# The order of outputs, transposes and copies in the second mixer of a two-block transformer kernel

## The chip, the cores and the metric

The kernel runs on one core of a Trainium2 chip. The metric is device time in microseconds of one execution. Before the change the median of three runs is 2345.12 us (2344.96 to 2345.4).

## The reference

Two transformer stacks run one after the other on one stream of 512 tokens of 1024 features. The first stack has two layers and also carries 256 context tokens, which are dropped after the last layer. Each of its layers has three attention mixers side by side, A, B and C, then a gate and an output product. Mixer B, the one that matters here, has 8 heads of 64 features. Each latent query sees a neighbourhood of 8 rows by 16 columns of latent keys with a learned bias, and all 256 context keys, in one softmax:

```
s_nb  = q . k_gathered + bias
s_ctx = q . k_context
p = softmax_f32(concat([s_nb, s_ctx]))
y = p[:neighbours] @ v_gathered + p[neighbours:] @ v_context
```

Context queries see only the context keys, and only in layer 0. The second stack (another attention, retention, convolution, pooling, and a feed-forward part) is not touched by the change.

## The kernel before, in words

Everything is written out by hand: each engine has its own loop over the same plan, and semaphores tie the queues together. A queue works strictly in its own order, so that order is the subject here.

Per layer, `project` makes the tiles of a mixer, then the mixer's attention runs over units. A unit is 128 queries of two heads. In mixer B a band unit has 512 keys a head (256 of context and a band of 256 latent ones), a context unit 256. `band_units` gives four band units for each of four pairs of heads, `context_units` two context units more in layer 0. That is 24 units in layer 0 and 16 in layer 1. A group is the units of one pair of heads: six and four.

`make_plan` turns the units into steps. The step of unit i names three of them: `unit` is i, `prev` is i-1, `old` is i-2. It also names up to one transpose of values for the coming pair of heads, which is done beside the transposes of `prev` (four, four and two tiles of 128 in three of the steps of a group; none in the last group). For `prev` the two halves of the partitions are transposed by pairs of 64-row matmuls: eight pairs for a band unit (16 matmuls), four for a context unit, and as many more as there are value tiles.

TensorE (`attention_pe`, L745) does in a step: `scores_pe` (matmuls at L621) of unit i; the transposes of unit i-1 (`turn_halves_pe`, L645, matmuls at L671), which first wait for both of its exponentials; and `outputs_pe` (L718) of unit i-2, which spreads the row weights (L715), then waits for the copy of the transposes and multiplies with the values (L730).

VectorE (`attention_dve`, L890): row minima with the bias added (L837, for context units L832), the copy of transposed probabilities (no unit of mixer B has any for VectorE), the reciprocal of the row sums (L855), the values copy (L888), then the product of outputs and weights (`outputs_dve`, L857: L862, L873).

ScalarE (`attention_act`, L940): in mixer B the two exponentials of unit i (`exponentials_act`, L928, activation at L937) come first and the copy of the transposes of unit i-1 (`turned_act`, L909, L926) last; `copies_last` is true where a unit has a set of two banks, which is mixer B alone. In mixers A and C the copy comes first. The exponentials write a buffer that the transposes of the unit before read, so they wait for them (L933 to L935). GpSimd only starts the loads of the bias behind the row minima (L958, L961).

Scores sit in three sets of two banks of PSUM in turn, transposes go into the banks of their own unit's scores, outputs have bank 1 and value transposes bank 0. The first two steps of a mixer run inside the last projection, and behind the last two there is one chunk of the next mixer's projection each (`latents_ahead`, L781, L790).

Of the kernel before, what the change touches and what calls it, by code (L numbers as in the profile page):

```python
# [226 lines left out]
def two_dit_blocks(nc, dram, kept, out):  # L227
    with ExitStack() as ctx:
# [478 lines left out]
        def spread_weights_pe(pe, u, o):  # L707

            if u["i"] >= 1:

                pe.wait_ge(y_done, u["u"] + o.u)
            pe.wait_ge(weight_ready, u["u"] + 1 + o.u)
            s, b = 2 * u["i"] % 4, u["out_bank"]
            for e in range(2):
                nc.tensor.matmul(bank(b, P, 2 * P)[rows_of(e)], weight[:, s + e:s + e + 1].to_broadcast([P, HD]), ident,  # L715
                                 start=True, stop=True, skip_group_check=True)

        def outputs_pe(pe, u, o):  # L718

            b = u["out_bank"]  # L720
            pe.wait_ge(values_taken, u["values_seen"] + o.w)
            spread_weights_pe(pe, u, o)
            for ev in u["events"]:
                if ev["by"] == "act":
                    pe.wait_ge(pt_by_act, ev["c"] + 1 + o.act)
                else:
                    pe.wait_ge(pt_by_dve, ev["c"] + 1)
                tiles = places(ev)
                for j, (at0, _, e, v) in enumerate(tiles):
                    ins = nc.tensor.matmul(bank(b, 0, P)[rows_of(e)], v, turned_slot(ev, at0 + P)[:, at0:at0 + P],  # L730
                                           start=ev["first"] and j < 2, stop=ev["last"] and j >= len(tiles) - 2,
                                           skip_group_check=True)
                ins.then_inc(pv_steps, 1)
# [11 lines left out]
        def attention_pe(pe, l, m, o, early):  # L745

            last = PHASES[m][1] - 1
            steps = plans[l, m][0]
            n_early = 2 if m == "B" else 1
            for step in steps[:n_early] if early else steps[n_early:]:  # L750
                u, prev, old = step["unit"], step["prev"], step["old"]
                i = u["i"] if u else None
                if i == 1 and m != "C":

                    pe.wait_ge(mod_taken, panels_through(l, m))
                if m == "B" and i == 2:

                    pe.wait_ge(proj_taken, NSEQ[l, last] + 1)
                if m == "A" and i == 1:

                    pe.wait_ge(proj_taken, NSEQ[l, last])
                if m == "B" and i == 2:

                    pe.wait_ge(values_taken, steps[0]["values"][1]["w"] + 1)
                if u and m in "AC" and u["p"] > 0:

                    pe.wait_ge(rope_done, rope_no(l, m, 1 + u["p"]) + 1)
                if u and not (m == "C" and i == 1):
                    scores_pe(pe, u, o)
                if u is None and old:  # L770
                    latents_ahead(pe, l, NEXT[m], 0 if prev else 1)
                if prev:
                    turn_halves_pe(pe, prev, [ev for ev in step["values"] if ev["halves"]])
                if m != "B" and i == 1:

                    pe.wait_ge(proj_taken, NSEQ[l, last] + 1)
                turn_values_pe(pe, step, o)
                if old:
                    outputs_pe(pe, old, o)

        def latents_ahead(pe, l, m, c):  # L781


            b = PHASES[m][0]
            k, n = NSEQ[l, b], main_no[IN1, l, b]
            if c == 0:
                pe.wait_ge(rest1_done, n + 1)
                pe.wait_ge(proj_taken, k - 1)
            for i, (w, h) in enumerate(((0, 0), (0, 1), (1, 0))):
                nc.tensor.matmul(bank(k % 2), split1[:, n % SPLIT1, w, c, :], hs1[:, h, c, 0:SEQ], start=c == 0 and i == 0, stop=False)  # L790
# [60 lines left out]
        def weights_dve(dve, u, o):  # L851

            s = 2 * u["i"] % 4
            dve.wait_ge(exp_done, 2 * u["u"] + 2 + o.u * 2)
            nc.vector.reciprocal(weight[:, s:s + 2], row_sum[:, s:s + 2]).then_inc(weight_ready, 1)  # L855

        def outputs_dve(dve, u, o):  # L857

            V = nc.vector
            dve.wait_ge(pv_steps, u["events"][-1]["k"] + 1 + o.k)  # L860
            a, f, d = bank(u["out_bank"], 0, P), y_weights[:, :], u["dst"]
            V.tensor_copy(f, bank(u["out_bank"], P, 2 * P))  # L862
            dve.drain()
            if len(d.shape) == 3:
                a, f = (x.rearrange("p (c r) -> p c r", r=ROWS) for x in (a, f))
            if "rest" in u:
                V.tensor_tensor(f, a, f, ALU.mult)
                dve.drain()
                V.tensor_copy(d, f)
                dve.drain()  # L870
                V.tensor_tensor(u["rest"], f, d.bitcast(F32), ALU.subtract).then_inc(y_done, 1)
            else:
                V.tensor_tensor(d, a, f, ALU.mult).then_inc(y_done, 1)  # L873

        def values_dve(dve, step, o, halves=False):

            for ev in step["values"]:
                if ev["halves"] != halves:
                    continue
                dve.wait_ge(turned, ev["t"] + 1 + o.t)  # L880
                if ev["after"]:

                    dve.wait_ge(pv_steps, ev["after"]["events"][-1]["k"] + 1 + o.k)
                to, of = ev["dst"], bank(ev["bank"], 0, P * len(ev["src"])).rearrange("p (t c) -> p t c", c=P)
                if ev["halves"]:
                    to = to.rearrange("p t (h q) -> p h t q", h=2)
                    of = bank(ev["bank"]).rearrange("p (h t q) -> p h t q", h=2, q=HD)[:, :, 0:len(ev["src"]), :]
                nc.vector.tensor_copy(to, of).then_inc(values_taken, 1)  # L888

        def attention_dve(dve, plan, o, behind_first=None):  # L890

            for step in plan:
                u, prev, old = step["unit"], step["prev"], step["old"]
                if u:
                    maxima_dve(dve, u, o)
                    if behind_first and u["i"] == 0:
                        behind_first()
                if prev:
                    turned_dve(dve, prev, o)
                    weights_dve(dve, prev, o)  # L900
                values_dve(dve, step, o, halves=True)
                if u and step["values_first"]:
                    values_dve(dve, step, o)
                if old:
                    outputs_dve(dve, old, o)
                if u is None or not step["values_first"]:
                    values_dve(dve, step, o)

        def turned_act(act, u, o):  # L909

            for ev in u["events"]:
                if ev["by"] == "act":
                    n = P * 2 * len(ev["tiles"])
                    if u["parts"]:
                        act.wait_ge(first_turned, u["x_no"] + 1)
                    else:
                        act.wait_ge(turned, ev["t"] + 1 + o.t)
                    if "slot_before" in ev:

                        act.wait_ge(pv_steps, ev["slot_before"]["k"] + 1 + o.k)  # L920
                    to, both = copy_of_turned(ev, n)
                    if u["parts"]:
                        nc.scalar.copy(to[:, 0], both[:, 0])
                        act.wait_ge(turned, ev["t"] + 1 + o.t)
                        to, both = to[:, 1], both[:, 1]
                    nc.scalar.copy(to, both).then_inc(pt_by_act, 1)  # L926
# [13 lines left out]
        def attention_act(act, plan, o, early=False):  # L940


            for step in plan:
                u, prev = step["unit"], step["prev"]
                copies_last = u and len(u["set"]) == 2
                if prev and not copies_last:
                    turned_act(act, prev, o)
                if u and not (early and u["i"] == 0):
                    exponentials_act(act, u, o)
                if prev and copies_last:  # L950
                    turned_act(act, prev, o)

        def attention_pool(pool, plan):

# [1588 lines left out]
        def _(pe):  # L2543
# [352 lines left out]
            for l in range(DEPTH):  # L2896
                for m in "ABC":
                    project(l, m)
                    attention_pe(pe, l, m, zero, False)
# [457 lines left out]
```

## Time and profile before

| what | us |
|---|---|
| median of three runs | 2345.12 |
| the profiled execution's own time | 2343.62 |
| its span, first to last instruction | 2341.8 |
| mixer B, layer 0, first transposes to last | 286.04 to 347.00 |
| mixer B, layer 1, second unit's transposes to last | 894.39 to 935.50 |

The profile is of one execution. PE is TensorE's matmuls and PEld its weight loads, which run ahead of them; DVE is VectorE, ACT ScalarE, POOL GpSimd. L and a number is a line of the kernel. Where TensorE has waited, its first matmul starts with its weight load; where it has not, the matmul follows the load by some 0.2 us.

### The profile page before, as it was taken

What the parts mean: (1) busy time and instruction counts of PE and PEld (TensorE: products, weight loads), DVE (VectorE), ACT (ScalarE), POOL (GpSimd) and SP (SyncE); (2) the same over time, 40 slices, a digit from 0 to 9 for tenths busy, and PEclk for the clock granted to TensorE, in tenths of its full rate; (3) what the DMA queues carried; (4) which work ended last, traced back from release to release, by engine and by line L of the source; (5) the groups of instructions that cost most, each with busy time, mean ns of one, the idle gap of its engine ahead of it and who ended that gap; (6) DMA issues with size and microseconds to landing.
All of it is one profiled execution on the core that took longest, in us unless ns stands there. A gap on an engine that the chain in (4) does not pass through costs nothing.

```text
span 2341.8 us, 39975 instructions
## 1 busy us (share of the span) xinstructions
PE 2300.3 (98%) x15942; PEld 1902.9 (81%) x15942; DVE 1401.3 (60%) x2818; ACT 1011.9 (43%) x1750; POOL 464.9 (20%) x291
## 2 busy tenths in 40 slices
PE   8999999999999999999999999999999999999998
PEld 7878878788888888888887688888888768888887
DVE  5878776787136766453388558847857755333333
ACT  5773375723247527653455442222235535221221
POOL 2102212022441131214752420000014232000001
PEclk9999999999999999999999999999999999999999
DMA  7303413042222151112241125445442112323222
GB/s 308 143 2 145 171 47 127 2 189 98 67 92 78 59 198 57 55 64 90 86 157 62 56 91 198 167 148 185 170 142 82 55 54 90 100 78 112 99 83 70
DMA packets 64201, 250.51 MB, mean 107 GB/s; under 512 B 7408, under 2 KB 9968, under 8 KB 54544
## 3 DMA queue, kind: packets, MB, share of 16 engines
q1 hardware_dynamic: 61216, 236.10, 29.0%
q0 software_dynamic: 2592, 11.54, 1.5%
q8 instruction: 126, 2.06, 0.4%
q14 instruction: 59, 0.48, 0.1%
q10 hardware_dynamic: 208, 0.33, 0.0%
HBM read 243.67 MB, written 4.19 MB: 106 GB/s over the span
## 4 chain that ended last, share of the span: by engine, by line
PE 89%; ACT 4%; DVE 3%; issue 2%; DVEq 1%; DMA 1%; POOL 1%; ACTq 0%; SPq 0%
PE ps L2948 41%; PE ps L2744 13%; PE ps L2729 8%; PE ps L2925 6%; PE ps L621 4%; PE ps L730 4%; ACT probs L937 3%; PE ps L671 3%; PE ps L715 1%; PE ps L2758 1%; PE ps L2965 1%; PE ps L2615 1%; DMA stage_low<-in_ada 1%; DVEq L820 1%; PE ps L2781 1%
## 5 line engine op out<-in xcount | busy, mean ns | idle before, releaser
L2948 PE MATMUL ps<-h_split,split_panels 128*128 128x512 f32 x2088 | 500.0, 394 | 1.2 <-ACT projected L1788 0.8
L2948 PEld LDWEIGHTS ps<-h_split,split_panels 128*128 128x128 f32 x2088 | 387.9, 188 | 92.8 <-issue 14.7
L1251 POOL TENSOR_TENSOR split_panels_first<-panels_first,split_panels_first 128x1024 fp32r<-128x1024 f32 (+2 forms) x100 | 220.8, 2208 | 728.9 <-ACT split_panels_first L1468 728.9
L2744 PE MATMUL ps<-h_split_first,split_panels_first 128*128 128x256 f32 (+1 forms) x1680 | 294.4, 337 | 0.0
L2744 PEld LDWEIGHTS ps<-h_split_first,split_panels_first 128*128 128x128 f32 x1680 | 258.3, 190 | 34.3 <-issue 1.0
L1269 POOL TENSOR_TENSOR probs_turned<-probs_turned,probs 128x512 f32<-128x512 f32 x30 | 40.0, 1332 | 764.3 <-ACT probs L1731 761.7
L2729 PE MATMUL ps<-h_split_first,split_panels_first 128*128 128x512 f32 (+1 forms) x900 | 190.5, 370 | 0.9 <-POOL h_split_first L1290 0.9
L2729 PEld LDWEIGHTS ps<-h_split_first,split_panels_first 128*128 128x128 f32 x900 | 156.3, 189 | 32.4 <-issue 3.0
L2243 DVE TENSOR_TENSOR split_panels<-panels,split_panels 128x1024 fp32r<-128x1024 f32 (+2 forms) x110 | 127.7, 1164 | 89.0 <-ACT split_panels L1493 88.9
L1920 ACT ACTIVATE probs<-ps 128x512 f32<-128x512 f32 x44 | 26.3, 599 | 349.8 <-PE ps L2948 349.7
L1493 ACT ACTIVATE split_panels<-panels 128x1024 fp32r<-128x1024 f32 (+2 forms) x149 | 144.7, 979 | 67.0 <-PE ps L2948 63.0
L2051 DVE SCALAR_TENSOR_TENSOR ps<-modulation_panels,silu_c,ps 128x256 f32<-128x256 f32 x312 | 145.5, 487 | 19.0 <-issue 1.3
L2948 PE MATMUL ps<-ffn_hidden_split,split_panels 128*128 128x512 f32 x624 | 145.7, 389 | 0.0
L621 PE MATMUL ps<-qkv 64*128 64x256 f32 (+1 forms) x1232 | 144.6, 360 | 0.3
L1468 ACT ACTIVATE split_panels_first<-panels_first 128x1024 fp32r<-128x1024 f32 (+2 forms) x104 | 102.5, 986 | 97.9 <-PE ps L2925 96.0
L937 ACT ACTIVATE probs<-ps,row_min 128x512 f32<-128x512 f32 (+6 forms) x192 | 122.2, 644 | 38.7 <-DVE row_min L837 29.0
L2948 PEld LDWEIGHTS ps<-ffn_hidden_split,split_panels 128*128 128x128 f32 x624 | 117.1, 188 | 24.3
L2925 PE MATMUL ps<-gated_rounded,split_panels_first 128*128 128x512 f32 x504 | 132.9, 356 | 0.0
L1281 POOL TENSOR_TENSOR split_panels<-panels,split_panels 128x1024 fp32r<-128x1024 f32 x39 | 94.5, 2423 | 169.3 <-ACT split_panels L1493 167.8
L621 PEld LDWEIGHTS ps<-qkv 64*128 64x128 f32 x1232 | 98.9, 186 | 25.9 <-issue 18.1
L671 PEld LDWEIGHTS ps<-matrices,probs 64*128 64x128 f32 x2048 | 80.6, 138 | 43.1 <-ACT probs L937 37.5
L1553 ACT ACTIVATE qkv<-ps 128x512 f32<-128x512 f32 x38 | 37.1, 975 | 167.2 <-PE ps L2744 118.0
(341 smaller groups left out, 3964.7 us busy)
## 6 DMA issues: line engine op xcount, KB each, us to landing
panels<-in_w SPq DMA_DIRECT2D x88, 512.0 KB, 3.7
modulation_panels<-in_ada SPq DMA_DIRECT2D x40, 1024.0 KB, 4.9
panels_first<-in_in SPq DMA_DIRECT2D x72, 512.0 KB, 4.8
late_modulation_panel<-in_ada SPq DMA_DIRECT2D x24, 1024.0 KB, 4.8
panels<-in_in SPq DMA_DIRECT2D x42, 512.0 KB, 3.7
panels_first<-in_out SPq DMA_DIRECT2D x32, 384.0 KB, 3.1
panels<-in_w SPq DMA_DIRECT2D x32, 384.0 KB, 3.5
panels<-in_w SPq DMA_DIRECT2D x32, 320.0 KB, 2.9
```

The lines of the kernel that those rows point to most:

```text
L621: last[e] = nc.tensor.matmul(scores_at(u, e, u["w"][e])[:, col:col + z - a], u["q"][e], u["k"][e][:, a:z], start=True, stop=True, skip_gro ...
L671: ins = [nc.tensor.transpose(to, src, ident[rows_of(half), HD * half:HD * half + HD]) for half, (to, src) in enumerate(two)]
L937: nc.scalar.activation(probs[:, u["probs_at"], e, 0:w], scores_at(u, e, w), ACT.Exp, bias=row_min[:, s:s + 1], scale=scale, accum_out=row_ ...
L1251: nc.gpsimd.tensor_tensor(flat1(n, 1)[:, s], raw1[:, n % RAW1, s], flat1(n, 0)[:, s].bitcast(F32), ALU.subtract).then_inc(rest1_done, 1)
L1468: A_(flat1(n, 0)[:, s], raw1[:, n % RAW1, s], ACT.Copy).then_inc(rounded1, 1)
L1493: A_(flat(n, l, 0), raw[:, n % RAW, 0:panel_size(n)], ACT.Copy).then_inc(rounded, 1)
L2051: ins = V.scalar_tensor_tensor(out=adding if c < KC - 1 else made[:, PAN * i:PAN * i + PAN], in0=w[:, c, :], scalar=v, in1=adding, op0=ALU ...
L2243: V.tensor_tensor(flat(n, l, 1), raw[:, n % RAW, 0:panel_size(n)], flat(n, l, 0).bitcast(F32), ALU.subtract).then_inc(rest_done, 1)
L2729: ins = mm(at0, split1[:, s, w, c, :], hs1[:, h, c, lo:e], start=c == 0 and i == 0, stop=c == KC - 1 and i == 2)
L2744: ins = mm(to, split1[:, s, w, c, :], hs1[:, h, c, lo:lo + n], start=c == 0 and i == 0, stop=c == KC - 1 and i == 2)
L2925: ins = mm(bank(OUT_BANKS[j][o % 2], 0, e), split1[:, n % SPLIT1, w, c, :], u[:, uc, lo:lo + e], start=uc == 0 and i == 0, stop=uc == MIXC ...
L2948: ins = mm(out, panel_of(n, l)[:, a, c - base, :], moving(b, c), start=first and i == 0 and j == 0, stop=last and i == len(chunks) - 1 and ...
```

## The change

In mixer B's steps three queues get another order. On TensorE the outputs of `old` come between the scores and the transposes. On VectorE the product of the outputs comes ahead of the values copy. On ScalarE the copy of the transposes comes ahead of the exponentials, as in the other mixers.

```diff
@@ attention_pe
                 if u is None and old:
                     latents_ahead(pe, l, NEXT[m], 0 if prev else 1)
+                if old and m == "B":
+                    outputs_pe(pe, old, o)
                 if prev:
                     turn_halves_pe(pe, prev, [ev for ev in step["values"] if ev["halves"]])
...
                 turn_values_pe(pe, step, o)
-                if old:
+                if old and m != "B":
                     outputs_pe(pe, old, o)
@@ attention_dve
                     weights_dve(dve, prev, o)
+                outputs_first = old and old["in_sets"] and len(old["set"]) == 2
+                if outputs_first:
+                    outputs_dve(dve, old, o)
                 values_dve(dve, step, o, halves=True)
...
-                if old:
+                if old and not outputs_first:
                     outputs_dve(dve, old, o)
@@ attention_act
-                copies_last = u and len(u["set"]) == 2
-                if prev and not copies_last:
+                if prev:
                     turned_act(act, prev, o)
                 if u and not (early and u["i"] == 0):
                     exponentials_act(act, u, o)
-                if prev and copies_last:
-                    turned_act(act, prev, o)
```

## Rows read from the trace of the kernel before

**Rows 1.** The page: busy us, share of the span, instructions of each engine.

```profile
PE 2300.3 (98%) x15942; PEld 1902.9 (81%) x15942; DVE 1401.3 (60%) x2818; ACT 1011.9 (43%) x1750; POOL 464.9 (20%) x291
```

**Rows 2.** By stretch: length, busy PE, PEld, DVE, ACT, POOL, granted clock, DMA.

```profile
396.00:480.00 84.00, 79.24 (x1136) 65.41 (x1137) 59.97 (x222) 55.48 (x124) 2.88 (x2) 1.00 0.05 17
284.00:346.00 62.00, 60.43 (x928) 49.37 (x926) 44.89 (x150) 48.34 (x116) 5.93 (x11) 1.00 0.18 52
886.00:935.00 49.00, 48.29 (x738) 41.45 (x735) 36.40 (x117) 36.88 (x79) 4.88 (x9) 1.00 0.20 59
```

**Rows 3.** Waits of PEld, mixer B in layer 0, then 1: total, times, longest.

```profile
PEld ps L671 <- ACT probs L937: 5.0, 11, 1.1
...
PEld ps L671 <- ACT probs L937: 1.5, 2, 1.1
```

**Rows 4.** Timeline, mixer B: group starts, and one step: start, us, engine, instruction.

```profile
300.73 0.73 PEld L621 LDWEIGHTS ps<-qkv 64*128 64x128 f32 x8 [0.17 <-issue]
...
316.77 0.73 PEld L621 LDWEIGHTS ps<-qkv 64*128 64x128 f32 x8 [0.17 <-issue]
...
338.47 0.73 PEld L621 LDWEIGHTS ps<-qkv 64*128 64x128 f32 x8 [0.17 <-issue]
...
340.02 0.20 PEld L715 LDWEIGHTS ps<-matrices,row_weight 128*64 128x64 f32 x4
...
341.15 0.68 ACT L937 ACTIVATE probs<-ps,row_min 128x512 f32<-128x512 f32 x1
341.26 0.30 PEld L621 LDWEIGHTS ps<-qkv 64*128 64x128 f32 x4 [0.17 <-issue]
```

**Rows 5.** Timeline, mixer B, the first two transposes, with values beside them.

```profile
286.04 0.14 PEld L671 LDWEIGHTS ps<-matrices,probs 64*128 64x128 f32 x1
...
288.81 0.13 PEld L671 LDWEIGHTS ps<-matrices,probs 64*128 64x128 f32 x1 [1.11 <-ACT probs L937]
...
289.73 0.20 PEld L715 LDWEIGHTS ps<-matrices,row_weight 128*64 128x64 f32 x4
...
289.93 0.69 ACT L937 ACTIVATE probs<-ps,row_min 128x512 f32<-128x512 f32 x1 [0.26 <-PE ps L671]
```

**Rows 6.** Timeline, mixer C in layer 0, where the copy stands ahead of the exponentials.

```profile
408.94 0.83 PE L671 MATMUL ps<-matrices,probs 64*128 64x64 f32 x20 [0.48 <-ACT probs L937]
...
409.84 1.01 ACT L926 COPY probs_turned<-ps 128x1024 f32<-128x1024 f32 x1 [0.95 <-PE ps L671]
...
410.75 0.70 ACT L937 ACTIVATE probs<-ps,row_min 128x513 f32<-128x513 f32 x1
...
411.43 0.69 ACT L937 ACTIVATE probs<-ps,row_min 128x513 f32<-128x513 f32 x1
...
412.26 0.71 PE L671 MATMUL ps<-matrices,probs 64*128 64x64 f32 x16
...
413.04 1.01 ACT L926 COPY probs<-ps 128x1024 f32<-128x1024 f32 x1 [0.83 <-PE ps L671]
```

**Rows 7.** Timeline, mixer B: context units and end in layer 0; layer 1.

```profile
345.13 0.47 ACT L937 ACTIVATE probs<-ps,row_min 128x256 f32<-128x256 f32 x1 [0.40 <-DVE row_min L832]
...
345.60 0.46 ACT L937 ACTIVATE probs<-ps,row_min 128x256 f32<-128x256 f32 x1
...
347.00 0.46 PE L671 MATMUL ps<-matrices,probs 64*128 64x64 f32 x8
...
347.39 0.20 PEld L715 LDWEIGHTS ps<-matrices,row_weight 128*64 128x64 f32 x4
...
347.53 0.59 ACT L926 COPY probs<-ps 128x512 f32<-128x512 f32 x1 [0.90 <-PE ps L671]
...
348.20 0.53 PEld L790 LDWEIGHTS ps<-h_split_first,split_panels_first 128*128 128x128 f32 x3 [0.17 <-issue]
...
894.39 0.27 PE L671 MATMUL ps<-matrices,probs 64*128 64x64 f32 x1 [0.71 <-ACT probs L937]
...
935.50 0.71 PE L671 MATMUL ps<-matrices,probs 64*128 64x64 f32 x16
```

## The prediction

> **What bounds the kernel now.** I read the busy shares first, then the busy time by stretch, then the waits inside the second mixer, then its timeline. TensorE is busy for 98% of the span [rows 1], and in the second mixer's two stretches for 60.43 of 62.00 us and 48.29 of 49.00 us, all at a granted clock of 1.00; ScalarE has 48.34 of 62 us of work there, so it is no bound by its sum [rows 2]. The only wait of TensorE that another engine causes in the mixer is that of the transposes for the exponentials: 5.0 us in 11 waits in the first layer, 1.5 us in 2 in the second [rows 3]. So before the change the stage is a chain of TensorE work with 6.5 us of holes, and 6.5 us is the most that filling these holes can bring. Any TensorE time that the change adds or removes here moves the end one for one, since what follows is TensorE-bound too.
>
> Names: S(i), T(i), O(i) are the scores, transposes and outputs of unit i on TensorE, E(i) its exponentials and C(i) the copies of its transposes on ScalarE. There are 24 units in layer 0 (four pairs of heads, each four band units of 512 keys and two context units of 256) and 16 in layer 1 (band units only), so 40 steps in all. The step of unit i has S(i), T(i-1), O(i-2) on TensorE and E(i), C(i-1) on ScalarE; after it, S(i), O(i-2), T(i-1) and C(i-1), E(i).
>
> **The change part by part.** It removes and adds no instruction; 40 steps are reordered on three queues, and no DMA is moved (POOL's band loads still follow the row minima).
>
> *TensorE's own price.* A band step without values beside it costs 341.26 - 338.47 = 2.79 us: S and T 1.55 us (338.47 to 340.02), spread weights and outputs 1.24 us (340.02 to 341.26) [rows 4]. The order of the three does not change that sum. T with twelve pairs (eight of probabilities, four of values) issues in 0.92 us [rows 5]; T with eight pairs by subtraction from S at about 0.76 in about 0.8, and tightly packed when it was waited for, about 0.64 (an estimate: 0.92 x 8/12).
>
> *ScalarE's order.* This is the part that decides. E(i) writes the same probs buffer that T(i-1) reads, and L933 to L935 already make E(i) wait for T(i-1); that wait is visible, ScalarE restarts 1.12 us after the first transpose (288.81 to 289.93) [rows 5]. Today C(i-1) comes behind E(i), off that path: the loop is T(i-1), E(i), T(i), 1.12 + 0.68 + 0.83 = 2.6 us, shorter than or equal to TensorE's own 2.8 to 3.2. With C(i-1) ahead of E(i) the loop is T(i-1), C(i-1), E(i), T(i), strictly serial. The third mixer already runs in this order, so its rows price each link [rows 6]: T with ten pairs to the copy 0.90 (408.94 to 409.84), with eight pairs 0.78 (412.26 to 413.04); copy of 1024 to the first exponential 0.91; first to second exponential of 513 columns 0.68; second exponential to the next transposes 0.83. Their sum there, 0.90 + 0.91 + 0.68 + 0.83 = 3.32, is exactly the distance of its two T (408.94 to 412.26). For context units the copy of 512 lasts 0.59 against 1.01 and the exponential of 256 0.47 against 0.69 [rows 6, 7]; I take copy to exponential 0.48, exponential to exponential 0.46, second exponential to transposes 0.61, and T with four pairs to the copy 0.53 (347.00 to 347.53) [rows 7].
>
> The loop from T(i-1) to T(i), for each unit i of a group in layer 0:
> - b0 after a context unit: 0.53 + 0.48 + 0.68 + 0.83 = 2.52
> - b1 and b2, T with twelve pairs (1.12 less the rounding): 1.11 + 0.91 + 0.68 + 0.83 = 3.53 each
> - b3, T with ten pairs: 0.90 + 2.42 = 3.32
> - c0: 0.78 + 0.91 + 0.46 + 0.61 = 2.76. Here another wait ends last: O(b3) now stands ahead of T(c0), and needs C(b3), which is done at 0.78 + 1.01 and about 0.07 for the signal; the outputs issue in 1.24 - 0.16 = 1.08, so T(c0) starts at 2.94
> - c1: 0.53 + 0.48 + 0.46 + 0.61 = 2.08
>
> A group of six: 17.92 us. Before it took 316.77 - 300.73 = 16.04 us [rows 4]. TensorE between two T has T, S, O: 0.64 + 0.76 + 1.24 = 2.64 (0.92 in place of 0.64: 2.92), below 3.20 and 3.53, so the loop rules and TensorE idles 0.5 to 0.6 us a band step. Does the wait of O(i-1) for C(i-1) add? It can start at 1.11 + 1.01 + 0.07 = 2.19 and issues to 3.27, still under 3.53; with eight pairs 1.86 + 1.08 = 2.94 under 3.20: no.
>
> Layer 0, from the first T: b1 to c1 of the first group 15.40; two whole groups 35.84; the last group has no values beside it, 2.52 + 3 x 3.20 + 2.94 + 2.08 = 17.14 (3.20 = 0.78 + 2.42). Sum 68.38. Before: 347.00 - 286.04 = 60.96 [rows 5, 7]. Cost +7.42.
>
> Layer 1: first group 3.53 + 3.53 + 3.32 = 10.38; two groups 3.20 + 10.38 = 13.58 each, 27.16; last group 4 x 3.20 = 12.80. Sum 50.34. Before: 2.77 for the first loop (286.04 to 288.81, the same instructions in layer 0) and 935.50 - 894.39 = 41.11 [rows 5, 7], 43.88. Cost +6.46.
>
> *TensorE's order* gives something back once per layer: O of the last unit but one no longer stands behind the last T. Layer 0: 348.20 - 347.39 = 0.81 [rows 7]. Layer 1: 1.24, less a new wait of the last outputs for the last copy, 0.78 + 1.01 + 0.07 against 0.64 + 0.9 of T and latents, 0.32: 0.92.
>
> *VectorE's order* is taken at nothing. O(i-2) is finished before T(i-1), so its product goes ahead of the values copy, which waits for T. The cover: S(i) starts 0.64 us after T(i-2), and both minima have served E(i) by 341.15 - 338.47 = 2.68 us after S began [rows 4]; E(i) now cannot begin before 3.20 + 0.78 + 0.91 = 4.9 after T(i-2), 4.25 after S(i). So up to 2.2 us of delay on VectorE is hidden. If that cover were gone, each late microsecond would add in its step. Bounds: 0 to +0.3 a group for the values copy of 0.69 us, which now stands last before the next minima, so 0 to +2 in all.
>
> Sum: 7.42 + 6.46 - 0.81 - 0.92 = +12.15 us on the profiled execution of 2343.62 us (span 2341.8 and 1.8 outside it). The median of the three timed runs is 1.5 us higher, 2345.12, so 2357.2 us.
>
> Bounds of the unknowns. The links come from another mixer with the same instructions; each is read to 0.05 us, and 38 loops with a common error of 0.1 make 3.8 us either way. The signal from copy to outputs (0.07) and the short-unit links are estimates worth 1 us. Low end 12 - 5.5, high end 12 + 6.
>
> A rule of the Trainium skill, beside this: "ScalarE: Activation LUTs", section "Rules for kernel authors", budgets about 0.3 us per activation and 0.83 ns an element, by which the copy of 1024 would take 1.15 us where the trace has 1.01 and lets the next instruction start after 0.91. By the page every loop would be some 0.24 us longer and the change would cost about 21 us; the measured row decides.
>
> **The rivals.**
> 1. *Faster: the holes are filled.* O(i-2) between S(i) and T(i-1) gives the exponentials 1.24 us more, and no wait seen is longer than 1.1 us. If the copies did not lengthen the way to E(i), all 6.5 us [rows 3] and both tails (0.81 + 1.24) would go: -8.6, 2336.5 us. For it: the waits are real and TensorE is the bound. Against: ScalarE's copy takes 0.91 of the 1.24, and it must wait for T(i-1), which itself has moved 1.24 later; the third mixer, in this order, waits at 408.94 and still takes 3.32 a step [rows 6]. It decides if the loop is under 2.8.
> 2. *No change.* Loop and TensorE's own time balance: that needs a loop of 2.9 us, 0.3 to 0.6 less than the third mixer shows. 2344 to 2346 us.
> 3. *Slower by more.* Copies and exponentials after each other cost more than in the third mixer, or the minima come late as well (the +2 above): a loop 0.24 longer, 38 x 0.24 = +9, 2366 us.
> 4. *TensorE's clock falls.* TensorE would idle about a sixth of the stage in holes of some 0.5 us. In the third mixer it is busy 79.24 of 84.00 us with its own such holes and the granted clock is 1.00 [rows 2]. If it fell to 1.2 GHz, TensorE's 2.8 us a step would be some 5.6, 40 x 2.3 = +92 over the stage, 2440 us. The Trainium skill, "TensorE: Matmul & The Clock Gate", section "A second HAM failure mode: psum-queue depth-cycling", tells of a kernel whose short idles between groups of matmuls made the clock swing; the trace, with such idles at full clock, speaks against it here.
>
> **How the numbers follow.** Forecast (slower by 7 to 18 us) 0.86; rival 1 0.05; rival 2 0.03; rival 3 0.05; rival 4 0.01. A measurement of this kernel tells about 0.2%, 4.7 us, from no change. Slower by over 0.2%: 0.92; within 0.2%: 0.03; faster by over 0.2%: 0.05. The range is the forecast's own with a little more at the low end, 2350.5 to 2363 us.
>
> **What would show it.** In the changed kernel's second mixer: the wait of transposes for exponentials grows from 6.5 us to some 20 (0.5 us a band step, 36 or so waits); ScalarE's idle before the copies is on TensorE's transposes and no longer on the minima; the copy starts 0.8 to 1.1 us after each T, and the distance of two T is 3.2 to 3.5 us; a group of six takes 17.9 us against 16.04. Mixers one and three, with the same queues as before, keep their lengths. I am wrong if a group takes under 16.0 us (then the copy was not on the loop), or if the waits of TensorE are on minima or on the copies (then the bound is another than I say).

## The result and the profile after

| | us |
|---|---|
| before, median of 5 runs | 2345.12 (2343.48 to 2345.47) |
| changed, median of 5 runs | 2355.29 (2355.08 to 2355.7) |
| ratio, 95% interval | 1.0046 (1.0035 to 1.0056) |
| span of the profiled execution | 2341.8 before, 2353.3 changed |

The change makes the kernel slower by 10.2 us; 12.1 were forecast. One execution of the kernel before, among those beside E5 to E8 below, took 4180.94 us at a granted clock of 0.82 and is left out of the ratios.

The page of the changed kernel shows next to nothing: TensorE is busy for the same 98% and its weight loads for the same 81%. The busy time of the matmuls even rose by 4.5 us with no matmul added; their ends are modelled, so the gaps below are read from the weight loads (PEld).

```profile
PE 2304.8 (98%) x15942; PEld 1898.4 (81%) x15942; DVE 1404.5 (60%) x2818; ACT 1011.5 (43%) x1750; POOL 465.0 (20%) x291
```

By stretch (length, then busy PE, PEld, DVE, ACT, POOL, granted clock, DMA), the second mixer of layers 0 and 1 in the changed kernel, against [rows 2]: TensorE idles 6.1 of 66 us and 3.1 of 47 us, where it was 1.6 of 62 and 0.7 of 49, at an unchanged clock.

```profile
284.00:350.00 66.00, 59.92 (x901) 44.41 (x902) 46.57 (x149) 47.26 (x111) 5.92 (x11) 1.00 0.16 46
893.00:940.00 47.00, 43.92 (x652) 34.55 (x652) 33.38 (x102) 31.96 (x67) 4.88 (x9) 1.00 0.19 58
```

The waits of layer 0's mixer in the changed kernel (who <- whom and line: total, times, longest), against [rows 3]: the transposes wait 23 times in place of 11, none longer than 0.5 us, and ScalarE's idle time is now that of its copies for the transposes, 24 times for 24 units. Before the change 10.2 us of ScalarE's idle time there were waits for minima; in layer 0 of the changed kernel there is none.

```profile
ACT probs_turned L931 <- PE ps L671: 10.0, 12, 1.1
ACT probs L931 <- PE ps L671: 9.9, 12, 1.1
...
PEld ps L671 <- ACT probs L942: 8.7, 23, 0.5
...
PEld ps L715 <- issue: 6.6, 19, 0.4
...
PEld ps L730 <- ACT probs_turned L931: 2.1, 4, 0.5
PEld ps L730 <- ACT probs L931: 2.1, 4, 0.5
```

The same wait in layer 1:

```profile
PEld ps L671 <- ACT probs L942: 7.4, 15, 0.5
```

Both layers together: 16.1 us in 38 waits, where the prediction had some 20 in about 36. The outputs (L730) wait for copies as well, 4.2 us in 8 waits in layer 0. The prediction called waits on the copies a sign that the bound is another; four of them are the wait into c0 that it had priced, and behind the other four the transposes still wait 0.50 us for the exponentials, so these do not end last.

The loop itself stands in the timeline (start, us, engine, instruction, idle time before it in brackets). This is one band step without values in the changed kernel, against [rows 4, 6]:

```profile
344.56 0.58 PEld L671 LDWEIGHTS ps<-matrices,probs 64*128 64x128 f32 x16 [0.50 <-ACT probs L942]
...
345.35 1.01 ACT L931 COPY probs_turned<-ps 128x1024 f32<-128x1024 f32 x1 [0.84 <-PE ps L671]
...
346.26 0.69 ACT L942 ACTIVATE probs<-ps,row_min 128x512 f32<-128x512 f32 x1
346.41 0.85 PEld L730 LDWEIGHTS ps<-probs_turned,mixed_first 128*64 128x64 f32 x16 [0.52 <-ACT probs_turned L931]
...
346.93 0.69 ACT L942 ACTIVATE probs<-ps,row_min 128x512 f32<-128x512 f32 x1
...
347.76 0.58 PEld L671 LDWEIGHTS ps<-matrices,probs 64*128 64x128 f32 x16 [0.50 <-ACT probs L942]
```

From transposes to copy 0.79, copy to first exponential 0.91, to the second 0.67, to the next transposes 0.83: 3.20 us. No minima stand in it, and no other wait of ScalarE.

Measured from one unit's transposes to the next (differences of such starts), with T, C, E, O, S as in the prediction:

| loop into unit | before | forecast | changed |
|---|---|---|---|
| b0 after a context unit | 2.75 | 2.52 | 2.52 |
| b1 of the first group, T with values | 2.77 | 3.53 | 3.63 |
| b1 of the next groups, T with values | 2.72 | 3.53 | 3.47 |
| b2, T with values | 2.94 | 3.53 | 3.47 |
| b3, T with fewer values | 2.74 | 3.32 | 3.32 |
| c0 | 2.25 | 2.94 | 2.87 |
| c1 | 2.64 | 2.08 | 2.12 |
| group of six | 16.04 | 17.92 | 17.77 |
| band units of the last group, no values | 2.34 to 2.94 | 3.20 | 3.19 or 3.20 |

First transposes to last, and last transposes to the next projection:

| | before | changed | difference | forecast |
|---|---|---|---|---|
| layer 0, T to T | 60.96 | 68.03 | +7.07 | +7.42 |
| layer 0, end | 2.90 | 2.09 | -0.81 | -0.81 |
| layer 1, T to T | 43.89 | 50.14 | +6.25 | +6.46 |
| layer 1, end | 4.11 | 2.87 | -1.24 | -0.92 |
| sum | | | +11.27 | +12.15 |

The difference of the two spans is 11.5 us. Outside the mixer the two profiled executions differ by -1.3 us in the first 35 us and +1.3 us at the seam of the layers, places that no edit touches. Mixers one and three keep their lengths.

### The profile page after: what moved, and what is told of

It reads as the page before. It is cut to its first block, busy times and chain, and to the rows that moved or that the text cites. A ratio compares the mean times of both kernels' runs of the same rounds, so it can differ in the third digit from the quotient of the medians.

```text
span 2353.3 us, 39975 instructions
## 1 busy us (share of the span) xinstructions
PE 2304.8 (98%) x15942; PEld 1898.4 (81%) x15942; DVE 1404.5 (60%) x2818; ACT 1011.5 (43%) x1750; POOL 465.0 (20%) x291
## 4 chain that ended last, share of the span: by engine, by line
PE 86%; ACT 6%; issue 3%; DVE 2%; DVEq 1%; DMA 1%; POOL 1%; ACTq 0%; SPq 0%
PE ps L2950 41%; PE ps L2746 12%; PE ps L2731 8%; PE ps L2927 6%; ACT probs L942 4%; PE ps L671 3%; PE ps L621 3%; PE ps L730 3%; PE ps L2967 2%; PE ps L2760 1%; PE ps L2617 1%; PE ps L715 1%; DMA stage_low<-in_ada 1%; DVEq L822 1%; PE ps L2783 1%
## 5 line engine op out<-in xcount | busy, mean ns | idle before, releaser
L671 PE MATMUL ps<-matrices,probs 64*128 64x64 f32 x2048 | 93.2, 228 | 20.9 <-ACT probs L942 19.0
```

What stands on the lines that cost most here:

```text
L671: ins = [nc.tensor.transpose(to, src, ident[rows_of(half), HD * half:HD * half + HD]) for half, (to, src) in enumerate(two)]
```

## Experiments

Each is told with its edit; times are medians beside runs of the kernel before on the same chip, and ratios have their 95% interval.

**E1, ScalarE's order alone.** On the kernel before:

```diff
-                copies_last = u and len(u["set"]) == 2
-                if prev and not copies_last:
+                if prev:
                     turned_act(act, prev, o)
                 if u and not (early and u["i"] == 0):
                     exponentials_act(act, u, o)
-                if prev and copies_last:
-                    turned_act(act, prev, o)
```

> The kernel before with ScalarE's order alone changed (mixer B's copy of transposes ahead of the next exponentials); TensorE and VectorE as before. Theory (serial loop transposes, copy, exponentials, transposes): the loop is there with TensorE's old order too. Layer 0 from first to last transposes about 67.6 us against 60.96 before, layer 1 about 50.1 against 43.9, and no gain at the ends since the last outputs stay behind the last transposes: 2345.1 + 6.7 + 6.3 = 2358 us, 2 to 3 us slower than the whole change. Rival (the cost is TensorE's new order, outputs waiting for copies ahead of the transposes): 2345 us, no change.

Measured 2359.65 against 2345.25 us, ratio 1.0068 (1.0054 to 1.0081). Between first and last transposes 69.61 and 50.19 us, ends 2.90 and 4.10 as before. The band loops are those of the whole change, 3.47, 3.48, 3.32, 3.20 in the same places. Waits of layer 0:

```profile
PEld ps L671 <- ACT probs L937: 15.7, 19, 2.0
ACT probs L926 <- PE ps L671: 11.6, 12, 1.1
ACT probs_turned L926 <- PE ps L671: 9.6, 12, 1.1
```

The rival is out: TensorE's new order is not needed for the loss. The 69.61 against the 67.6 expected lies in the short units: into b0 the loop is 2.75 and into c1 2.39, where I had carried over 2.52 and 2.08. There TensorE's own work, with outputs still behind transposes, is the longer of the two (the kernel before has 2.75 and 2.64). So TensorE's and VectorE's parts of the change, taken together, give some 4 us back (2359.65 to 2355.29).

**E2, VectorE's order alone.** The middle part of the diff, on the kernel before.

> The kernel before with VectorE's order alone changed (product of the outputs ahead of the values copy). Theory: covered; the values copy ends 0.5 us later and the next minima up to 0.2 us later, inside the slack of the transposes in steps of 2.9 to 3.2 us: 2345 us, 0 to +1. Rival (VectorE's order carries part of the cost): +2 or more.

Measured 2349.92 against 2345.25 us, ratio 1.0024 (1.0014 to 1.0034): slower by 4.7 us. The rival was right and I was not. T to T grows by 2.46 us (63.42) in layer 0 and by 2.87 (46.76) in layer 1, all of it behind transposes that have values beside them. In a whole group of layer 0 the loop into b1 goes from 2.72 to 3.21 and into b2 from 2.94 to 3.69, and the one into b3 falls from 2.75 to 2.47. The step into b2 in its timeline:

```profile
304.39 0.73 PEld L621 LDWEIGHTS ps<-qkv 64*128 64x128 f32 x8 [0.17 <-issue]
...
304.51 0.29 DVE L862 COPY weights_of_y<-ps 128x128 f32<-128x128 f32 x1 [0.60 <-PE ps L730]
...
305.08 0.68 DVE L888 COPY mixed_first<-ps 128x512 f32<-128x512 f32 x1
...
305.88 0.13 PEld L671 LDWEIGHTS ps<-matrices,probs 64*128 64x128 f32 x1 [0.76 <-ACT probs L940]
```

The name in the bracket is misleading: the exponentials had ended at 305.14 (304.46 and 0.68), the transposes start only 0.12 us after the values copy of the step before (305.08 and 0.68). All value transposes share one bank of PSUM, and `turn_halves_pe` waits for it ahead of all its pairs. The copy is late because the product of the outputs now stands ahead of it, and starts only at 304.51, when TensorE has done the outputs, which in this run still stand behind the transposes. In the whole change the outputs stand ahead of the transposes, the product is done in time, and the values copy starts 1.06 us after its transposes (288.33 to 289.39), 2.4 us before the next ones (291.80):

```profile
289.39 0.69 DVE L890 COPY mixed_first<-ps 128x512 f32<-128x512 f32 x1 [0.25 <-PE ps L671]
```

No loop there is longer than ScalarE's links explain. The whole change without VectorE's part was not run. I had looked for the delayed minima and not for the bank.

**E3, TensorE's and VectorE's order without ScalarE's.** The changed kernel with the old `attention_act`.

> The changed kernel with ScalarE's order put back (exponentials first, copy last); TensorE and VectorE keep the new order. Theory: ScalarE's order is what costs in the change, but it can't be left out once outputs stand ahead of transposes: then the loop is transposes, exponentials, copy, outputs, transposes: 1.11 + 1.35 + 1.08 + 1.08 = 4.62 us for a unit with values beside it, 4.29 without, 23.4 a group of six against 17.8 with the whole change. Layer 0 about 89.6 us between first and last transposes, layer 1 about 66.7: 2345.1 + 28.7 + 22.8 - 1.7 = 2395 us. Rival (outputs between scores and transposes only fill the holes, 6.5 us of them): 2337 to 2345 us.

Measured 2395.02 us, ratio 1.0219 (1.0205 to 1.0233), as expected (four executions, 2393.53 to 2399.6). 89.54 and 66.26 us between first and last transposes; loops of 4.55, 4.40 and 4.27 us. One of them:

```profile
361.69 0.58 PEld L671 LDWEIGHTS ps<-matrices,probs 64*128 64x128 f32 x16 [0.17 <-issue]
...
362.53 0.69 ACT L942 ACTIVATE probs<-ps,row_min 128x512 f32<-128x512 f32 x1 [1.92 <-PE ps L671]
...
364.94 0.85 PEld L730 LDWEIGHTS ps<-probs,mixed_first 128*64 128x64 f32 x16 [1.49 <-ACT probs L931]
...
365.96 0.57 PEld L671 LDWEIGHTS ps<-matrices,probs 64*128 64x128 f32 x16 [0.17 <-issue]
```

Exponentials wait for transposes, outputs wait for the copy behind the exponentials, transposes wait in TensorE's queue behind the outputs. So the parts of the change belong together: TensorE's and VectorE's orders without ScalarE's cost 50 us, ScalarE's alone 14, all three 10. TensorE's order alone was not run. VectorE has no link in the loop above, so I put the 50 us down to TensorE's order; that is argued and not shown by a run of its own.

**E4, half the copy.** The changed kernel, and in `turned_act`:

```diff
                     to, both = copy_of_turned(ev, n)
...
+                    if u["in_sets"] and len(u["set"]) == 2:
+                        to, both = to[:, 0], both[:, 0]
                     nc.scalar.copy(to, both).then_inc(pt_by_act, 1)
```

> The changed kernel, all orders as changed, but in mixer B ScalarE copies only one of the two halves of each block of transposed probabilities (512 in place of 1024 elements a partition, 256 in place of 512); the other half of each row keeps older content, so mixer B's outputs are wrong in part. Theory: the copy is a link of the loop, so each loop of a band unit falls by 0.42 us, 3.47 to 3.04, 3.32 to 2.89, 3.20 to 2.77, until TensorE's own work of 2.7 to 3.0 a step is the bound: layer 0 about 59.8 us between first and last transposes (68.0 with the whole copy), layer 1 about 43.5 (50.1); 2355.3 - 14.8 = 2340 us, below the kernel before. Rival (ScalarE's copy is off the path and TensorE's order with its new gaps of 0.33 us before the spread weights is the cost, 40 x 0.33 = 13 us): 2354 to 2355 us, no change.

Measured 2342.35 against 2345.25 us, ratio 0.9991 (0.9982 to 1.0), 12.9 us below the changed kernel where 14.8 were expected (60.89 and 44.26 us between first and last transposes, not 59.8 and 43.5). Against the kernel before that is 2.9 us faster, with an interval that just reaches 1. Loops of 3.08, 2.90 and 2.80 us:

```profile
337.90 0.57 PEld L671 LDWEIGHTS ps<-matrices,probs 64*128 64x128 f32 x16 [0.17 <-ACT probs L944]
...
338.39 0.74 PEld L621 LDWEIGHTS ps<-qkv 64*128 64x128 f32 x8
...
338.68 0.59 ACT L933 COPY probs<-ps 128x512 f32<-128x512 f32 x1 [0.86 <-PE ps L671]
...
339.46 0.20 PEld L715 LDWEIGHTS ps<-matrices,row_weight 128*64 128x64 f32 x4 [0.33 <-issue]
...
340.70 0.58 PEld L671 LDWEIGHTS ps<-matrices,probs 64*128 64x128 f32 x16 [0.17 <-ACT probs L944]
```

A copy shorter by 0.42 us takes 0.40 off each band loop (3.20 to 2.80), and the wait of the transposes falls from 0.50 to 0.17 us: the copy is a link. The rows also price TensorE's new order by itself. The spread weights start 0.33 us late behind scores (338.39 + 0.74 to 339.46), but what follows the transposes starts sooner: the scores 0.49 us after them here (337.90 to 338.39), the spread weights 0.80 us after them in the kernel before (to 340.02 in [rows 4]):

```profile
339.22 0.73 PEld L671 LDWEIGHTS ps<-matrices,probs 64*128 64x128 f32 x16
```

The step is 2.80 us against 2.79 in [rows 4]. So in a plain step the order costs nothing, as the prediction had it.

**E5 to E7, two buffers for the probabilities.** The scratch of mixer B is laid out anew (two blocks of probabilities of 1024 columns, two slots of turned ones), and exponentials wait for the transposes of two units back:

```diff
-        u["probs_at"], u["probs_of"] = (0, before) if sets else (i % 2, two_back)
+        u["probs_at"], u["probs_of"] = (0, before) if sets and len(sets) == 2 else (i % 2, two_back)
...
+        of_both = flat_probs[:, 0:2048].rearrange("p (i e n) -> p i e n", i=2, e=2)
...
+                if len(ev["set"]) == 2 and ev["own"] == 1:
+                    return flat_probs[:, 2048:2048 + n]
```

E5, on the changed kernel:

> The changed kernel with two buffers for mixer B's probabilities in turn, so that the exponentials of a unit no longer wait for the transposes of the unit before, only for those of two before. Theory: ScalarE's queue order holds the loop by itself, since the copy, which waits for these transposes, stands ahead of the exponentials: band loops stay 3.47 and 3.20 us, 2355.3 us, no change against the changed kernel. Rival (the shared buffer is what ties exponentials to transposes): the loop opens and the time falls toward TensorE's own work, 2340 to 2346 us.

Measured 2355.74 us; against the kernel before (2344.31) the ratio is 1.0047 (1.0034 to 1.0061). First to last transposes of layer 0 are again 68.03 us, with every loop within 0.01 us of the changed kernel's. The queue order alone holds the loop. That corrects the prediction in one point: it named the shared buffer as the tie; in the changed kernel it is a second tie that is never the last.

E6, on the kernel of E3:

> The run with TensorE's and VectorE's new order and ScalarE's old one (2395 us), now with two buffers for the probabilities. Theory: here ScalarE starts the exponentials ahead of the copy, so the shared buffer was a link of the 4.3 to 4.6 us loop; without it two steps take scores to exponentials 3.4, copy 1.08, outputs 1.08, transposes 0.64 us = 6.2, that is 3.1 us a step (3.25 with values): about 4 us above the kernel before, 2347 to 2353 us. Rival (the loop passes by the copy and not by the buffer): stays at 2390 or more.

Measured 2350.58 us, ratio 1.0029 (1.0019 to 1.0039): 44 us come back with the buffer. Band steps of 2.93 to 3.15 us, where 3.1 to 3.25 were expected. So with TensorE's new order, which of the two ties counts depends on ScalarE's queue: with the copy behind the exponentials it is the buffer, with the copy ahead of them it is the copy.

E7, on the kernel before:

> The kernel before with two buffers for the probabilities, nothing else. Theory: its transposes wait for exponentials that wait for minima, and only few exponentials wait for transposes (2.1 us in layer 0), so 2344 to 2345.5 us, no change that can be told. Rival (the loop of transposes and exponentials, 2.6 us, bounds the kernel before): 2 us or more faster.

Measured 2343.76 against 2344.31 us, ratio 0.9998 (0.9989 to 1.0007), no change.

**E8, outputs of three units back.** An attempt to beat both, from the kernel of E3:

```diff
+    deep = sets is not None and len(sets) == 3
...
-        step = dict(unit=u, prev=before, old=two_back, values=[], values_first=values_second)
+        old = two_back if not deep else flat[i - 3][1] if i > 2 else None
+        step = dict(unit=u, prev=before, old=old, values=[], values_first=values_second)
...
-        weight = sb("row_weight", [P, 4])
+        weight = sb("row_weight", [P, 6])
```

> A version to beat both: TensorE's new order (outputs between scores and transposes), but the outputs are those of the unit three back, with a third slot for turned probabilities, ScalarE's old order (exponentials first, copy last), VectorE's outputs ahead of values, values of the next pair of heads one step later. No outputs wait for a copy of the same step, so the loop is transposes, exponentials, transposes, 2.6 us, under TensorE's own 2.8 to 3.2, and scores are 4 to 5 us ahead of their transposes, more than the 3.5 us that minima and exponentials take. Theory: the holes of 6.5 us in the kernel before close, 2339 to 2341 us. Rival (TensorE's new order has a price of its own, 0.33 us before each spread of weights after scores, 40 times): 2345 to 2355 us.

Measured 2346.14 against 2344.31 us, ratio 1.0008 (0.9999 to 1.0016): the expectation failed, and the time lies in the rival's range. A group of six did fall, to 15.63 us from 16.04, and T to T in layer 0 from 60.96 to 60.46; but layer 1 rose from 43.89 to 44.14, and each end by 0.88 us (3.78 and 4.99). PEld's waits in layer 0's mixer and the end of it:

```profile
PEld ps L736 <- issue: 6.7, 18, 1.0
PEld ps L690 <- ACT probs L963: 3.0, 11, 1.3
```

```profile
351.05 0.23 PEld L736 LDWEIGHTS ps<-matrices,row_weight 128*64 128x64 f32 x4 [1.02 <-issue]
```

The first hole, before the second unit's transposes, has no outputs to fill it in any order (the loop is 2.75 there, 2.77 before), and it was 1.1 of layer 0's 5.0 us and 1.1 of layer 1's 1.5. And two outputs now stand directly behind each other at the end, with one bank for outputs, so that the weights of the last wait 1.02 us, put down to issue (in the kernel the spread of the weights waits for VectorE's product of the unit before). The two ends cost 2 x 0.88 us.

Between the ends both layers together gained only 0.25 us of the 6.5 expected. In a whole group of layer 0 the transposes waited 1.2 us for exponentials before the change and no longer do, yet the group fell by only 0.41 us, so some 0.8 us a group are new. What grew is the gap before the spread weights, from 0.5 to 2.0 us a group (0.33 us, six times); sooner scores and tighter transposes gave a part back. So the rival was right in kind: outside plain steps (E4) TensorE's new order seems to have a price of its own. This run has other edits beside it and does not separate them.

**E9, the order of mixer B in all mixers.** On the kernel before, `copies_last = bool(u)`.

> The kernel before with its order of mixer B (exponentials first, copy of the transposes last) on ScalarE in mixers A and C too. These have two sets of score banks, not three, so the scores of the next unit wait for the copy of the unit before. Theory: the order that is right in B is wrong there: scores, minima, exponentials, copy and the next scores become one serial loop, about 5.6 us a band step in C against 3.3 to 3.5, and about 2.5 us more a unit in A: roughly 80 steps by 2.3 = +190 us, 2530 us. Rival (copies ahead of exponentials cost A and C what they cost B, 0.3 to 0.6 us a step): 25 to 40 us faster, 2305 to 2320 us.

One execution each: 2511.25 against 2345.3 us, +166. Unit to unit in mixer C's band steps mostly 5.6 to 6.8 us (once 7.2) where it was 3.3 to 3.9, in mixer A mostly 6.6 to 6.8 (some 7.7) where it was 3.8 to 4.4; mixer B's loops are to 0.01 us what they were. A step of C in this run:

```profile
521.68 0.69 ACT L937 ACTIVATE probs<-ps,row_min 128x513 f32<-128x513 f32 x1 [4.03 <-DVE row_min L837]
...
522.36 0.68 ACT L937 ACTIVATE probs<-ps,row_min 128x513 f32<-128x513 f32 x1
...
523.02 1.01 ACT L926 COPY probs<-ps 128x1024 f32<-128x1024 f32 x1
524.14 1.22 PEld L621 LDWEIGHTS ps<-qkv 64*128 64x128 f32 x18 [1.93 <-issue]
```

With two sets of banks the next scores (524.14) start when the copy is done (524.03), and their minima must pass before anything else of ScalarE's. With three sets, in B, the same copy frees a bank that is not needed for a step. The granted clock fell too in parts of this run (last section), and its share in the 166 us is not separated.

## Why the prediction was right

*The loop.* Right, link by link. The prices from the third mixer carried over to the second within 0.1 us a loop; E4 shows that the copy is a link of it, and E1 that ScalarE's order alone makes it.

*The wait of O(b3) for its copy, into c0.* Right: 2.87 against 2.94. O(b3) stands 0.52 us for its copy, and the transposes behind it then have no more than the 0.17 us of a queue that does not wait, where those of a band unit have 0.50. (The 0.52 us at 346.41 above is O(b2), behind which the transposes still wait.)

```profile
349.61 0.85 PEld L730 LDWEIGHTS ps<-probs,mixed_first 128*64 128x64 f32 x16 [0.52 <-ACT probs L931]
...
350.63 0.33 PEld L671 LDWEIGHTS ps<-matrices,probs 64*128 64x128 f32 x8 [0.17 <-ACT probs L942]
```

*TensorE's order at nothing in a plain step.* Right for that step (E4, 2.80). The 0.33 us in front of the spread weights was not foreseen; it is made up by scores that start sooner. In groups with context units E8 points to a price of some 0.8 us a group; in the change it is hidden, since the loop is longer than TensorE's work.

*The ends.* Layer 0 exact. Layer 1 gave back 1.24 and not 0.92: the last outputs do wait for the last copy and start 1.85 us after the last transposes, as priced (0.78 + 1.01 + 0.07). But I set that against the start of the spread weights (1.54 us, 949.49), and outputs start some 0.17 us behind these anyway. So the term of 0.32 us was mis-sized: the wait that is left is 0.1 us, and the next projection follows the outputs after 1.02 us where it was 1.11.

```profile
947.95 0.57 PEld L671 LDWEIGHTS ps<-matrices,probs 64*128 64x128 f32 x16 [0.50 <-ACT probs L942]
...
949.49 0.20 PEld L715 LDWEIGHTS ps<-matrices,row_weight 128*64 128x64 f32 x4 [0.36 <-issue]
...
949.80 0.85 PEld L730 LDWEIGHTS ps<-probs,mixed_first 128*64 128x64 f32 x16
950.82 1.24 PEld L2731 LDWEIGHTS ps<-h_split_first,split_panels_first 128*128 128x128 f32 x9 [0.17 <-issue]
```

*VectorE's order at nothing.* Right in the whole change as far as the loops show, and for too narrow a reason: I followed the minima alone. E2 shows a price of 4.7 us for the same edit, through the bank of the value transposes, where the outputs stand behind the transposes.

*The size.* 12.1 forecast, 10.2 measured, 11.3 in the two profiles' mixers. Most loops with values were over-priced by 0.06 us (1.11 + 0.91 + 0.68 + 0.83 against 3.47), ten of them, 0.6 us: T with twelve pairs reaches its copy in 1.06 us (288.33 to 289.39). The four loops into c0 were over-priced by 0.07 each, and layer 1's end by 0.3. Against these the first loop of each layer was under-priced by 0.10 (its T had not waited and took 1.22 us to the copy, 284.70 to 285.92) and those into c1 by up to 0.04, so part of the closeness is errors that cancel. The last 1.1 us, between the mixers' sum and the medians, lies within the spread of the two sets of runs.

*The rule on ScalarE's price.* The copy of 1024 took 1.01 us and let the exponential start after 0.91 here too. The Trainium skill's budget ("ScalarE: Activation LUTs", "Rules for kernel authors") is stated there for an activation whose bias is a pointer operand, and the copy, whose row reads ps alone, has none: the prediction's 21 us stretched the rule. The exponential of 512 columns has such a bias (row_min); an estimate by that budget is 0.3 + 512 x 0.00083 = 0.72 us, and the trace is near it with 0.69. *The clock* stayed at 1.00 in the mixer with some 40 waits of up to 0.5 us, so the rival on it is out for this change.

## What to carry to other kernels

Before an instruction is moved ahead on a queue, write down the ring that it closes: what it waits for, what stands behind it, and who feeds what it waits for. Here a copy that had been free behind the exponentials cost 0.4 us a step ahead of them (6.25 us in the 15 loops of layer 1), though ScalarE was busy for only three quarters of the time. In this kernel the copy goes last where there are three sets of score banks and first where there are two, and each order in the other's place costs 14 (E1) and 166 us (E9). That the number of sets is the reason is read from who waits for whom; no run changed the number of sets in one mixer. Price a ring from a stage that already runs in the new order; and try edits that belong together as a group, for ScalarE's order alone, and the other two without it, each cost more than all three.

## What the runs showed that I had not expected

In all 22 steps of layer 0 where the spread weights follow scores in the changed kernel, they started 0.33 to 0.41 us after the last weight load of the scores; the profile puts 17 of these gaps down to issue and 5 to VectorE's values copy. Behind a chunk of the next projection the gap is 0.36 to 0.42 us in both kernels, behind transposes it was 0.07 to 0.13 before the change. What makes it was not tried. And in E9, where TensorE was busy for 130.13 of 180 us in mixer A and the start of the projection behind it, the granted clock of the stretch fell to 0.95, that is, it was for part of it at the lower of its two levels (1.2 in place of 2.4 GHz), and to 0.91 in a stretch with 83.32 of 100 us busy:

```profile
95.00:275.00 180.00, 130.13 (x1474) 113.51 (x1474) 105.33 (x252) 74.14 (x154) 11.98 (x5) 0.95 0.10 36
...
400.00:500.00 100.00, 83.32 (x740) 74.03 (x736) 51.79 (x139) 47.41 (x87) 13.86 (x6) 0.91 0.21 75
```

The second stretch is two stages: up to 450 us TensorE was busy for 50.00 of 50 us and the clock was 1.00, and from there, in mixer C, for 33.32 of 50 us and it was 0.83. In mixer B of the changed kernel, where no gap between weight loads was longer than 0.52 us, it did not fall. What decides between the two was not tried.
